# Norm factors from tokens in partitions, an earlier evacuation in two last heads, and one more weight split on VectorE in a decoder step

## The reference

```python
h = rmsnorm(x, norm_mix_g)
proj = h @ w_in
a = pool_mix(...)            # causal pooling, 4 groups
b = retention_mixer(...)     # 4 heads of width 256, with a group norm over each head's output
x = x + concat([a, b]) @ w_out
x = x + mem_attn(rmsnorm(x, norm_mem_g), mk, mv, w_mq, w_mo)     # 4 heads, 256 memory tokens
x = x + peer(rmsnorm(x, norm_ffn_g), peer_wq, subkeys, u, v)     # 8 heads, top 16 of 16384 experts
y = rmsnorm(x, norm_final_g)
def rmsnorm(x, g):
    return x * rsqrt(mean(x * x, axis=-1) + 1e-6) * g
```

## Time and profile before

| | us |
|---|---|
| median of 3 runs | 4602.15 |
| lowest and highest run | 4591.28, 4606.64 |
| the profiled execution, its time | 4598.67 |
| its span, first to last instruction | 4596.9 |
| mean granted clock of PE | 0.985 of full speed |
| PE busy | 4377.5 (95% of the span) |
| POOL, DVE, ACT busy | 2814.5, 2453.6, 1534.4 |

### The profile page before, as it was taken

How to read it: one execution, slowest core, us unless ns; L and a number is a source line. 1 busy time by engine, 2 the same in 40 slices (tenths; PEclk the granted TensorE clock), 3 DMA queues, 4 the chain that set the end, 5 groups by cost and what they waited for, 6 DMA issues and landing times.

```text
span 4596.9 us, 75376 instructions
## 1 busy us (share of the span) xinstructions
PE 4377.5 (95%) x28747; PEld 4138.6 (90%) x28747; DVE 2453.6 (53%) x3198; ACT 1534.4 (33%) x1928; POOL 2814.5 (61%) x1440
## 2 busy tenths in 40 slices
PE   7999999899999989999999998999999999999997
PEld 6899989799888978888888898999999999999997
DVE  3632333413102155555555865777777777777656
ACT  4422222222222234444443553333333333333333
POOL 6933222243222447777777787787888788886653
PEclk9999999999999999999999999999999999999998
DMA  6643333344554245555656568999999899999853
GB/s 217 201 102 102 108 107 109 107 142 144 193 190 177 82 156 183 183 183 182 183 182 184 163 205 317 364 357 346 355 358 358 311 362 358 356 357 347 316 196 138
DMA packets 491785, 1032.01 MB, mean 225 GB/s; under 512 B 55680, under 2 KB 281088, under 8 KB 458880
## 3 DMA queue, kind: packets, MB, share of 16 engines
q1 hardware_dynamic: 314384, 590.67, 38.8%
q0 software_dynamic: 45056, 268.60, 15.0%
q10 hardware_dynamic: 132208, 170.85, 10.6%
HBM read 935.26 MB, written 94.73 MB: 224 GB/s over the span
## 4 chain that ended last, share of the span: by engine, by line
issue 35%; POOL 28%; PE 25%; DMA 7%; DVE 3%; ACT 2%; POOLq 0%; SPq 0%; ACTq 0%; DVEq 0%
POOL WS L450 25%; PE PS L564 13%; PE PS L939 13%; DMA RAW<-in_vE 6%; POOL AR L474 2%; ACT WS L970 1%; POOL ROWS L484 1%; DVE AR L1550 0%; DVE AR L1844 0%; DVE AR L1576 0%; DMA AR<-gel 0%; DMA pmap<-ROWS 0%; DMA AR<-in_vE,AR 0%; DVE AR L1828 0%; PE PS L906 0%
## 5 line engine op out<-in xcount | busy, mean ns | idle before, releaser
L564 PE MATMUL PS<-HL,WS 128*128 128x288 f32 (+2 forms) x16896 | 2392.9, 303 | 75.0 <-DVE HL L1587 19.7
L564 PEld LDWEIGHTS PS<-HL,WS 128*128 128x128 f32 x16896 | 2348.9, 190 | 97.2 <-issue 45.6
L450 POOL TENSOR_TENSOR WS<-RAW,WS 128x1024 fp32r<-128x1024 f32 x602 | 1477.8, 2466 | 1437.6 <-ACT WS L970 1434.5
L970 ACT ACTIVATE WS<-RAW 128x1024 fp32r<-128x1024 f32 x602 | 616.4, 1055 | 1156.0 <-PE PS L564 436.7
L939 PE MATMUL PS<-WW,WS 128*128 128x320 f32 x6144 | 927.6, 313 | 57.0 <-POOL WS L450 47.9
L939 PEld LDWEIGHTS PS<-WW,WS 128*128 128x128 f32 x6144 | 910.3, 190 | 73.7 <-issue 38.1
L853 PE MATMUL PS<-WS,HL 128*128 128x512 f32 x3072 | 700.7, 390 | 2.9 <-POOL WS L450 2.9
L853 PEld LDWEIGHTS PS<-WS,HL 128*128 128x128 f32 x3072 | 575.8, 188 | 121.8 <-POOL WS L450 3.4
L450 POOL TENSOR_TENSOR WS<-CS,WS 128x1024 fp32r<-128x1024 f32 x200 | 491.2, 2456 | 135.3 <-ACT WS L970 133.3
L1901 DVE SCALAR_TENSOR_TENSOR PS<-ROWS,AR,PS 128x2048 f32<-128x2048 f32 x206 | 483.6, 2347 | 10.2 <-DMA ROWS<-in_vE,AR 9.8
L1916 DVE TENSOR_TENSOR AR<-AR,PS 128x320 f32<-128x320 f32 x512 | 247.6, 484 | 324.1 <-PE PS L939 323.0
(11 more groups left out here) (169 smaller groups left out, 2470.3 us busy)
## 6 DMA issues: line engine op xcount, KB each, us to landing
RAW<-in_uT SPq DMA_DIRECT2D x256, 512.0 KB, 4.7
RAW<-in_w_lin SPq DMA_DIRECT2D x218, 512.0 KB, 3.5
CS<-in_uT SPq DMA_DIRECT2D x128, 512.0 KB
AR<-in_uT SPq DMA_DIRECT2D x128, 512.0 KB
RAW<-in_vE SPq DMA_DIRECT2D x128, 512.0 KB, 6.5
CS<-in_vE SPq DMA_DIRECT2D x64, 512.0 KB
AR<-in_vE SPq DMA_DIRECT2D x64, 512.0 KB
AR<-in_w_lin SPq DMA_DIRECT2D x46, 512.0 KB
```

The source lines that it names most:

```text
L450: pool.tensor_tensor(WS[:, k, 1, :], raw(k, many, late), WS[:, k, 0, :].bitcast(F32), ALU.subtract)\
L564: ins = mm(to, WS[:, slot + hf, wp, k * P:(k + 1) * P], x, start=first and (wp, xp) == (0, 0), stop=last and wp == 1, skip_group_check=True)
L970: copy = lambda out, in_, **kw: act.activation(out, in_, ACT.Identity, **kw)
```

## The change

**The first part** concerns the norms k = 0, 1, 3 and 4 (k = 2 stays). `token_sums` makes the same sums with NACC as the stationary operand: 96 tokens by 1 column, six times (for the memory tokens 128 by 1, twice), so a token is a partition and its group a column. Epsilon, root, reciprocal and Newton step then work on 96 by 6 (128 by 2) numbers. DVE multiplies them into an identity, which gives 96 rows by 576 columns with one block-diagonal entry in each column, and `spread_factors` multiplies that by the matrix of 1/2048 on PE (the factors were multiplied by 2048 in the Newton step), which leaves the factors in all partitions, in PSUM. For k = 0 and 1 DVE copies them to SBUF, for k = 3 and 4 the scaling reads PSUM. PE waits in `spread_factors` for DVE.

**The second part**, in the last head of the retention, puts the copies of the samples, the outputs and the state behind blocks 2, 4 and 7 of `split_early` on ACT. PE makes the means first, then one round of states, the variances and the other round inside `out_early` (m = 0), with the states in banks 4, 5, 2 and 3, and `out_early` (m = 1) waits for all states. DVE centres the outputs after nine low parts, and makes the second four states after the variance's epsilon, ahead of the reciprocal.

**The third part**, in the last head of the attention, lets the loads into QM wait for `qz_done` and a new signal `qm_free`, given by PE when the products of the queries with the prompt's keys are done.

**The fourth part** moves one more low part of each quad, k = 13 (in the rest k = 5), from POOL to DVE, where it stands behind the sum of block 4, and counts semaphores anew. In the first quad DVE makes the low part of k = 7 two instructions earlier.

```diff
+LOW_DVE, LOW_TAIL = (3, 7, 11, 13, 15), (3, 5, 7)
...
+            def token_sums(k, n=T):
+                w = token_rows(n)
+                pe.wait_ge(S["sq_used"], 16 * (k + 1))
+                for c in range(n // w):
+                    ins = mm(PS[0:w, 512 * 6 + c:512 * 6 + c + 1], NACC[:, w * c:w * (c + 1)], ONES[:, 0, 0:1],
+                             start=True, stop=True, skip_group_check=True)
+                ins.then_inc(S["sum_done"], 1)
+
+            def spread_factors(j, n=T):
+                w = token_rows(n)
+                pe.wait_ge(S["rd_ready"], j + 1)
+                part = n if n == MEM else HALF
+                for c in range(n // part):
+                    ins = mm(bank(6 + c, part), ONES[0:w, 0, :], NT[0:w, 1, part * c:part * (c + 1)], start=True, stop=True)
+                ins.then_inc(S["rb_done"], 1)
...
+                def last_states(k2):
+                    if k2 == 0:
+                        pe.wait_ge(S["o_evac"], h + 1)
+                        pe.wait_ge(S["spr_evac"], h + 1)
+                        means()
+                    elif k2 == 2:
+                        pe.wait_ge(S["km_done"], h + 1)
+                        pe.wait_ge(S["lin_evac"], h * 8 + (B_HEAD + 5 + 3))
+                        state_round(0, LAST_BANKS)
+                    elif k2 == 4:
+                        variances()
+                    elif k2 == 5:
+                        pe.wait_ge(S["sst_new"], h * SB + 4)
+                        state_round(1, LAST_BANKS)
...
-                    act.wait_ge(S["ks_used"], h * SB + SB)
+                    act.wait_ge(S["qz_done"], h + 1)
+                    act.wait_ge(S["qm_free"], h + 1)
...
                 dve.wait_ge(S["sd_ready"], k + 1)
-                link(dve.reciprocal(NRS[:, 0:n], NRS[:, 0:n]))
-                newton(NRS[:, 0:n], NVAR[:, 0:n], NACC[:, 0:n])
+                link(dve.reciprocal(r, r))
+                newton(r, v, t, out, float(D))
+                tt(NT[0:w, 1, 0:n].rearrange("p (c x) -> p c x", c=per), IDENT[0:w, 0:w].unsqueeze(1).to_broadcast([w, per, w]),
+                   wide(out, w), ALU.mult).then_inc(S["rd_ready"], 1)
+                dve.wait_ge(S["rb_done"], min(k, 2 if k < 4 else 3) + 1)
+                if k < 2:
+                    link(dve.tensor_copy(NRS[:, 0:n] if n == MEM else halves(NRS), bank(6, n) if n == MEM else pair(3)))
...
                 def after(d):
-                    if d in (1, 9):
-                        low_last(H_UV + 16 * i + 11 + d // 2)
+                    if d in (1, 4, 9):
+                        low_weights(H_UV + 16 * i, 11 + d // 2)
```

248 lines of the change are left out of this document (153 added, 95 removed), and 2 rows, old and new, of the table names.

## The result

The changed kernel took 4619.45 us (median of 6 runs, 4616.59 to 4625.42) and the kernel before, beside it, 4597.32 (6 runs, 4591.28 to 4606.64): a ratio of 1.0048, 95% interval 1.0035 to 1.0062. It is 0.5% slower; 4624 had been forecast, and 1.0058 as a ratio to that median. The profiled execution of the changed kernel has a span of 4614.8 us, against 4596.9.

A forecast was written before the change was run, and what follows sets the result against it. PE, busy 95% of the span, was taken to bound the kernel, plus its waits. Loop +45, norms -2.6, retention -14 and attention -3 make +25 on 4598.67: 4624 us, own range 4605 to 4643 (50%), 8 in 10 within 4562 to 4662.

The forecast's parts named there:

- The moved low part: Quads, k = 13 on DVE: block 8 starts 1.5 us later in each of 25 quads, 37 us.
- Rivals A and B: Quads: A, DVE's low part works as meant, total 4549, 10%; B, transfer comes some 1.5 us sooner, total 4579, 15%.
- The clock: Quads: waits near 1.9 us sometimes cost 1.5 us more at the lower clock; half that in 11 quads, 8 us.
- rival C: Quads: the clock falls in nearly every quad, another 30 us, total 4654, 15%.
- The first quad: Earlier low part of k = 7 can shorten an up-half wait, but the down half gives that back: 0.
- The retention: Last head: the 14.47 us wait before the transposes goes, less 0.5: -14 us, between -7 and -17.
- The attention: Last head: earlier loads into QM shorten PE's 6.07 us wait: -3 us, between -1 and -6.
- The norms: Small chains and one-column sums: k = 0 -2.5, k = 1 +6.0, k = 3 -2.3, k = 4 -3.8 us, together -2.6.
- The product with the identity at k = 0: Norm k = 0: DVE beside POOL can hold this product for up to a low part of 2.42 us.
- the -0.1: Norm k = 0: the gain if DVE and POOL lock each other out for a whole instruction, instead of -2.5 us.
- the 45: Loop of quads: the moved low part and the clock together, +45 us, between -30 and +75.
- rival D: Early copies don't pay, another wait replaces the 14.47 us, and k = 1 costs 9: sum +38, total 4637, 10%.

The follow-up runs named there:

- e6: The changed kernel with the loads of k = 12 and 13 halved, so the output isn't the layer's: 4569.61 us, ratio 0.9927.
- e1: The changed kernel without its fourth part (POOL makes the low part of k = 13 again): 4571.69 us, ratio 0.9936.
- e2: The kernel before with the fourth part of the change alone: 4650.10 us, ratio 1.0105.
- e3: The changed kernel with DVE's low part of k = 13 behind the sum of block 5 instead of block 4: 4625.98 us, ratio 1.0060.
- e4: The changed kernel with the low part of k = 13 behind sum 5 and gathered rows six to nine behind sums 7, 10, 12, 14: 4552.56 us, ratio 0.9888.
- e5: The changed kernel with only gathered rows six to nine moved, behind sums 7, 10, 12 and 14: 4605.90 us, ratio 1.0009.
- e8: e4 with the first quad's low part of k = 7 put back in its old place: 4551.52 us, ratio 0.9892.
- e9: e1 with gathered rows six to nine moved behind sums 7, 10, 12 and 14: 4577.18 us, ratio 0.9944.
- e12: The edits of e7 and e8 together on e4: 4546.69 us, ratio 0.9884.
- e7: e4 with the spread of norm k = 1 behind the first two blocks of the memory values: 4546.98 us, ratio 0.9884.
- e10: e7 with the last heads of the retention and the attention as in the kernel before: 4572.18 us, ratio 0.9949.
- e11: e7 with all four norms as in the kernel before: 4567.81 us, ratio 0.9936.

## Why the prediction was right, point by point

**The moved low part: right in mechanism and in each step.** The prediction put block 7 at 3223.0 and block 8 at 3225.75 in the quad of the earlier trace rows, 2.75 and 5.50 us after the high part starts at 3220.25. Measured were 2.77 and 5.42, in this quad and in most of the 24. It is a sum of rows of before, in the order in which DVE meets them. The price per quad was 1.42 us, not 1.5, and was paid in 24 quads of the loop as 34 us (37 for 25 had been forecast). The example quad served well by some luck: 4.00 us before is more than the mean of 3.81. The condition on which it rested, that the high part ends later than 10.7 us after the start of the down half, is met by all 25 quads of the kernel before, and e6 shows what happens where the transfer is 2 us earlier: 44 us less in the 24 quads. Rivals A and B fall with that, since the transfer came no sooner in the changed kernel.

**The clock: too much.** Eight us more were forecast for the loop, and rival C wanted 30. The granted clock of the 24 quads averages 0.995 in the kernel before and in e1 and 0.994 in the changed kernel, so that at most 7 and 9 us were lost to it: 2 more. Rival C's mechanism exists all the same, in the kernels beside it: at most 19 us were lost in e2 and 22 in e3.

**The first quad: wrong, and the largest miss.** The term was 0; the changed kernel lost 11.8 us there against e1 (15.8 us ahead of before instead of 27.6). With the same stages ahead, the second down half starts at 2892.8 to 2898.2 in the kernels with the low part of k = 13 on DVE (e3, e4, e5, e6, e8 and the changed one), at 2886.4 and 2887.5 in those with it on POOL (e1, e9). The step that failed is "but the down half behind it is released by POOL as in the earlier trace rows, which gives that back: 0". The traces show two things in its place.

First, the new counts of the semaphores delay the first quad's first load. The load of k = 0 waits for the count of POOL's low parts that the code works out for k = -4 (`split_uv(0, -4)`): H_UV + 2 with POOL's twelve low parts a quad, H_UV + 3 with eleven (H_UV is a constant of the code), so one low part of the stage ahead more. The changed kernel (SP's load, ACT's high part of k = 1, the copies queued behind it on ACT, and PE, which needs them):

```profile
2771.29 7.23 SPq L455 DMA_DIRECT2D RAW<-in_uT  x2
...
2781.90 1.06 ACT L1031 ACTIVATE WS<-RAW 128x1024 fp32r<-128x1024 f32 x1 [4.46 <-DMA RAW<-in_uT]
...
2782.86 1.91 ACT L1031 ACTIVATE ROWS<-PS 128x512 f32<-128x512 f32 x2
...
2784.02 2.05 PE L966 MATMUL PS<-AR 128*128 128x128 f32 x8 [4.81 <-ACT ROWS L1031]
```

And e1, which is 1.7 us ahead there and has no such wait of PE:

```profile
2763.51 6.35 SPq L455 DMA_DIRECT2D RAW<-in_uT  x2
...
2774.40 1.06 ACT L1031 ACTIVATE WS<-RAW 128x1024 fp32r<-128x1024 f32 x1 [2.61 <-DMA RAW<-in_uT]
```

Counted from PE's product 300 ahead of the first down half, this load is issued 3.8 us after it in all eleven kernels with the low part on DVE and 2.2 us before it in the other three (before, e1, e9). The eleven have a wait of PE of 4.4 to 5.1 us for ACT's copies, the three have none, and the next 100 products take 20.8 to 21.7 us in the eleven and 14.2 in the three.

Second, the earlier low part of k = 7 costs time instead of none. From the same product to the second down half the nine kernels that have both it and the low part of k = 13 on DVE took 128.4 to 132.1 us, e8 and e12, with the latter alone, 125.0 and 125.8, and before, e1 and e9 120.6 to 122.3. So of the changed kernel's 10.1 us over e1 in this stretch (130.7 and 120.6) some 3 to 5 are left of the late load and the low part of k = 13, and the rest goes with the low part of k = 7 (3.4 and 4.6 us in the pairs e4, e8 and e7, e12). The 1.7 us ahead of it lie in code that e1 and the changed kernel share, where single traces vary by more. No kernel with the old wait for the first load and the rest as changed was run, so the two pieces of the first part aren't separated.

**The retention: 16.7 instead of 14.** From the first product behind the head's last wait (862.17 before, 864.22 after) to the product after the early blocks (921.31 and 906.62) are 59.1 and 42.4 us. The mechanism is the one named. Too cautious were the 0.5 us for what is late next: that chain shortened as well (3.60 instead of 5.47). e10 puts the two heads together at 15 to 21 us, against 17 forecast.

**The attention: 3.04 instead of 3.** The earlier trace rows have 6.07, the row above 3.03.

**The norms.** k = 0: 28.97 to 26.77, **-2.2** instead of -2.5. k = 3: from the sums to the first scaled block 6.7 us (1614.93 to 1621.62) instead of 8.2; before it was 10.5, so **-3.8** instead of -2.3. The term that was too large is that of the twelve sums: 2.08 us, not 3.4, since a product of one column costs 0.17 us at the low clock, not 0.29: the weight load is less than a third of the 0.57 us that one over 288 columns took the earlier trace rows, where I took half. k = 1: from the sums to the memory values 6.04 us; before 1.49 (137.58 to 139.07 in its trace), so **+4.5** instead of +6, by the same term. k = 4: 6.7 us from the sums to the scaling, 9.4 before, **-2.8** instead of -3.8: sums and spread ran at the low clock (2.07 and 2.29 us), where I had taken the full one's 1.24 for the spread from the earlier trace rows. The scalings with the factors in PSUM are no slower, as forecast: 3.71 us for five, 11.76 for 16 before. Together -4.3 where -2.6 were forecast.

The product with the identity at k = 0 was not held by POOL. It starts at 20.89 together with POOL's low part and takes 0.42 us; what is held is the pair of scaled blocks behind it, 3.19 us for two. By the Trainium skill, SBUF — State Buffer, section "SBUF: two separate sides", the engine that starts first has the shared ports for its whole instruction; the trace agrees with the 3.19 us, and the -0.1 that was worked out for a DVE held off didn't come true, since DVE came no later than POOL.

**The sum.** Norms and heads gave 29.7 us instead of 20 (spans of the kernel before and e1), and the fourth part cost 47.6 instead of 45 (spans of e1 and the changed kernel). The net is 18 us by these spans and 22 by the medians (4619.45 and 4597.32), and was forecast as 25. Inside the 47.6, 32.6 fall on the 24 quads, 11.8 on what lies before them and 3.3 behind. So two misses of the 45 offset each other: 12 us up to the second quad that were costed at nothing, and some 12 of the loop that weren't paid. Of the 10 us more at the front 2.7 are the retention's and 1.7 the norms'. The rest I can't name: the kernels with the same stages ahead are 22 to 28 us ahead of the kernel before at the product 300 ahead of the first down half, and the named gains add up to 21 there. The total is nearer than its terms, and that is luck. A slip without weight: rival D's terms add up to +42, not +38.

## What to carry to other kernels

Moving work to an idler and faster engine says nothing until its place in that engine's order is costed: an instruction that waits for a late transfer makes everything behind it on an in-order engine as late as the transfer. List what stands between the event and what the bounding engine needs, with durations (here 1.2 + 0.4 + 2.3 + 0.5), compare it with the chain that is replaced (0.4 + 2.4), and move first what nobody waits for (the 2.35 us row) out of the chain; here the same move brought 19 us in one order with the rows moved too (e4 against e1; the rows alone brought nothing, e9) and cost 48 in the other. Gains of separate places in one trace could be added here to within some 7 us; undoing them singly gave the heads back as read and the norms only within a wide margin. Where counts of semaphores change, look at the seam between two stages: one count more held a load, and through the in-order queue of ACT PE, for 5 us.

## What the runs showed of the hardware

- **What a wait costs beyond itself.** Over 192 quads of eight kernels (before, e3, e4, e5, e7, e8, e9, e12) I took the period less 57.27 us, the shortest, and less the waits in the down half. With a longest wait under 1.6 us the rest is 0.3 us on average, and 3 of 145 quads are over 0.8. With 1.6 to 1.8 us it is 0.9 (3 of 7), with 1.8 to 2.5 us 1.4 (14 of 21), with more than 2.5 it is 2.2 (19 of 19). This is the lower of PE's two clocks: of the 40 quads with a wait of 1.8 us or more, 31 have a mean granted clock below 0.985. In the changed kernel and in e2, whose waits are split in two, it is 5 of 12 and 9 of 13 such quads, so it isn't shown that the split helps. The first row is a quad of the changed kernel with 2.33 us ahead of block 7 at no cost (windows: engines' busy times, then PEclk, DMA share, GB/s); the second has 2.73 us, and its clock is lower:

```profile
3140.00:3201.00 61.00, 57.33 (x385) 56.48 (x386) 44.84 (x40) 19.25 (x25) 45.19 (x29) 1.00 0.91 342
3379.95:3441.94 61.99, 58.62 (x385) 57.70 (x385) 45.12 (x41) 19.03 (x25) 45.24 (x28) 0.97 0.90 337
```

- **Products of one column aren't free.** At the lower clock (granted 0.50) twelve PE instructions over 128 by 96 weights and one column took 2.08 us, 2.00 of them with weight loads (PEld), nearly as much as four over 288 columns (2.29).
- **The same loop code varies by 12 us.** The 24 quads of e4, e7, e8, e10, e11 and e12, with the same code in the loop, took 1401.7, 1389.6, 1398.0, 1393.0, 1393.7 and 1397.2 us in their profiled executions; a difference of 10 us between two single traces of this loop means nothing by itself.
